# Residual update of eight chunks: five adds on GpSimd and three on VectorE, instead of four and four

## The reference

```python
def _rmsnorm(x, g):
    xf = x.astype(jnp.float32)
    y = xf * lax.rsqrt(jnp.mean(xf * xf, axis=-1, keepdims=True) + EPS)
    return (y * g.astype(jnp.float32)).astype(x.dtype)

def _pre(x, g, mod, k):
    return _rmsnorm(x, g) * (1.0 + mod[:, 3 * k + 1][:, None]) + mod[:, 3 * k][:, None]

def _post(x, y, g, mod, k, weight):
    return x + weight * mod[:, 3 * k + 2][:, None] * _rmsnorm(y, g)

x = _post(x, _swiglu(_pre(x, g[0], mod_lat, 0), ffn1_gu[l], ffn1_down[l]), g[1], mod_lat, 0, 0.5)
```

## Time and profile before

| | us |
|---|---|
| median of 3 runs | 2696.45 (2695.09 to 2696.85) |
| the profiled execution | 2699.14 |
| span of its trace | 2697.3 |
| PE busy | 2620.2 (97%) |
| DVE busy | 1641.0 (61%) |
| POOL busy | 827.6 (31%) |
| ACT busy | 718.1 (27%) |

### The profile page before, as it was taken

One profiled execution on the slowest core, in us unless ns is written; L12 is line 12 of the kernel. 1 busy time (PEld: TensorE's weight loads), 2 busy tenths in 40 slices (PEclk: granted clock), 3 DMA queues, 4 the chain that ended last, 5 costly groups with the idle time before them and its releaser, 6 DMA issues.

```text
span 2697.3 us, 40977 instructions
## 1 busy us (share of the span) xinstructions
PE 2620.2 (97%) x17108; PEld 2446.3 (91%) x17108; DVE 1641.0 (61%) x2293; ACT 718.1 (27%) x1022; POOL 827.6 (31%) x1292
## 2 busy tenths in 40 slices
PE   6999999999999999999999999999999999999998
PEld 4999999998969899999999899999999868788886
DVE  5688878867563677667666733443434684644444
ACT  5212212123314422112112412122113414322222
POOL 1268876832140200000000248677651051000001
PEclk9999999999999999999999999999999999999999
DMA  9534443453464143443442322222223556233331
GB/s 333 141 118 160 142 155 130 164 178 128 127 182 143 40 133 119 132 125 117 132 127 85 92 83 84 92 87 92 92 94 128 174 166 188 71 94 101 95 94 63
DMA packets 340466, 337.19 MB, mean 125 GB/s; under 512 B 52529, under 2 KB 311225, under 8 KB 336697
## 3 DMA queue, kind: packets, MB, share of 16 engines
q1 hardware_dynamic: 279224, 204.07, 25.8%
q10 hardware_dynamic: 51840, 77.07, 8.5%
q0 software_dynamic: 9216, 53.42, 5.3%
HBM read 290.02 MB, written 44.50 MB: 124 GB/s over the span
## 4 chain that ended last, share of the span: by engine, by line
PE 87%; DVE 7%; ACT 2%; issue 2%; POOL 1%; DMA 1%; SPq 0%; DVEq 0%; ACTq 0%; POOLq 0%
PE ps L464 78%; PE ps L1630 2%; POOL xT L1198 1%; PE ps L1655 1%; DVE hL L1403 1%; DVE tmpN L1399 1%; PE ps L1218 1%; PE ps L1233 1%; PE ps L613 1%; ACT wH L449 1%; PE ps L1644 1%; DMA xin<-in_x_dram 1%; PE ps L965 1%; PE ps L984 0%; DVE adaW L571 0%
## 5 line engine op out<-in xcount | busy, mean ns | idle before, releaser
L464 PE MATMUL ps<-hH,wH 128*128 128x384 f32 (+1 forms) x2928 | 1013.0, 346 | 6.6 <-DVE hL L1403 3.8
L464 PE MATMUL ps<-hH,wL 128*128 128x384 f32 (+1 forms) x2928 | 1004.9, 343 | 0.0
L464 PE MATMUL ps<-hL,wH 128*128 128x384 f32 (+1 forms) x2928 | 1004.5, 343 | 0.0
L456 DVE TENSOR_TENSOR wL<-raw,wH 128x1024 fp32r<-128x1024 f32 x300 | 389.3, 1309 | 476.1 <-ACT wH L449 474.7
L464 PEld LDWEIGHTS ps<-hH,wH 128*128 128x128 f32 x2928 | 550.1, 188 | 32.4 <-DVE hL L1403 6.3
L464 PEld LDWEIGHTS ps<-hH,wL 128*128 128x128 f32 x2928 | 550.1, 188 | 18.3
L464 PEld LDWEIGHTS ps<-hL,wH 128*128 128x128 f32 x2928 | 550.3, 188 | 17.8
L464 PE MATMUL ps<-midH,wH 128*128 128x384 f32 (+1 forms) x1232 | 424.9, 345 | 3.7 <-DVE yT L877 3.3
L449 ACT ACTIVATE wH<-raw 128x1024 fp32r<-128x1024 f32 x300 | 310.7, 1050 | 423.6 <-PE ps L464 406.8
L464 PE MATMUL ps<-midH,wL 128*128 128x384 f32 (+1 forms) x1232 | 422.2, 343 | 0.0
L464 PE MATMUL ps<-midL,wH 128*128 128x384 f32 (+1 forms) x1232 | 422.1, 343 | 0.0
(11 more groups left out here) (271 smaller groups left out, 2295.9 us busy)
## 6 DMA issues: line engine op xcount, KB each, us to landing
raw<-in_ffn_gu_dram SPq DMA_DIRECT2D x176, 512.0 KB, 3.8
adaW<-in_w_ada_dram ACTq DMA_DIRECT2D x40, 1536.0 KB, 6.9
raw<-in_ffn_down_dram SPq DMA_DIRECT2D x88, 512.0 KB, 3.6
x_d<-xT POOLq DMA_DIRECT2D x4, 3072.0 KB, 10.5
xT<-x_d POOLq DMA_DIRECT2D x4, 3072.0 KB, 11.5
W_d<-gW POOLq DMA_DIRECT2D x16, 512.0 KB, 3.6
VT_d<-gVT ACTq DMA_DIRECT2D x16, 512.0 KB, 3.0
raw<-in_w_in_dram SPq DMA_DIRECT2D x16, 512.0 KB, 5.4
```

The costliest lines, as they stand in the source:

```text
L456: nc.vector.tensor_tensor(wL[:, n % SPLIT_SLOTS, :], raw[:, n % RAW_SLOTS, :], wH[:, n % SPLIT_SLOTS, :].bitcast(f32), ALU.subtract).then_ ...
L464: ins = nc.tensor.matmul(dst, a, b, start=first and n == 0, stop=last and n == 3 * len(pairs) - 1)
```

## The change

The list of POOL's chunks gets a fifth. `DVE_CHUNKS` follows from it.

```diff
-    POOL_CHUNKS = (0, 1, 2, 3)
+    POOL_CHUNKS = (0, 1, 2, 3, 4)
     DVE_CHUNKS = tuple(m for m in range(KC) if m not in POOL_CHUNKS)
```

## The result

| | before | after |
|---|---|---|
| median of 4 runs, us | 2696.11 (2695.09 to 2696.85) | 2728.97 (2727.46 to 2729.49) |
| the profiled execution | 2699.14 | 2728.87 |
| its span | 2697.3 | 2727.1 |
| mean granted clock of TensorE | 0.996 | 0.990 |

The change makes the kernel slower: ratio 1.0121, 95% interval 1.0104 to 1.0139. That is some 33 us between the medians and 29.7 between the two profiled executions, where 4.7 were forecast. That is far outside the predicted range.

A forecast was written before the change was run, and what follows sets the result against it. With POOL's residual adds on the path to a PE busy 97%, the terms 3.40 + 0.81 + 0.52 = +4.73 us put the median at 2701.2 us, from 2696.45; the range was 2698.3 to 2705.5.

The forecast's parts named there:

- What bounds the kernel: PE is busy 97% of the span; POOL's residual adds in the norm stages are on the path to the end.
- off the path: Rival: POOL's fifth add costs the norm stages nothing, the end gives 0.60 back at best; 2695.9 us, chance 0.05.
- The handover between the two adders: Adds of DVE and POOL exclude each other; the waiting engine goes next, a blocked POOL instruction ending 1.71 after its release.
- The first four norm stages, 768 columns: POOL's add of chunk 4 goes first by 0.04; PE's row sums come 0.85 later per stage, +3.40 in all.
- DVE first in all stages: Rival: DVE's chunk 5 goes ahead of POOL's chunk 4, +1.71 per 768-column stage; 2704.6 us, chance 0.24 (some or all).
- The second mixer's stage: Norm stage of 512 columns: DVE goes first, POOL's chunk 4 follows, PE's row sums start later: +0.81.
- the end of the program: PE waits for all eight chunks; DVE first, then POOL's chunk 4, then DVE's last two adds: +0.52.
- POOL first everywhere: Rival: POOL goes first in every stage, as it has no wait between its adds; +4.35, 2700.8 us, chance 0.14.
- No blocking: Rival: the two engines' adds do not block each other; +3.11, 2699.6 us, chance 0.10.
- The list of what would show it wrong: POOL's fifth add much over 1.8, a falling granted clock, or ACT's square of chunk 4 less than 0.8 later.

The follow-up runs named there:

- e4: Changed kernel, but DVE waits once for all eight scaled chunks ahead of its three adds, instead of before each; 2704.2 us, ratio 1.0025.
- e1: Changed kernel, but DVE waits after each of its adds until that add has finished; 2715.22 us, ratio 1.0063.
- e6: Changed kernel, but DVE's weight split waits until POOL has done its five adds; 2721.74 us, ratio 1.0095.
- e7: Changed kernel, but DVE's second add waits for all eight scaled chunks and its third for nothing; 2724.99 us, ratio 1.0103.
- e5: Changed kernel with 16 filler matmuls instead of one on PE after chunk 3 in the 768-column stages; 2717.56 us, ratio 1.0075.
- e9: Changed kernel, one wait for all eight scaled chunks ahead of DVE's adds, POOL's fifth add held back by waits; 2713.31 us, ratio 1.0058.
- f3: Changed kernel, pause put before the last chunk's scaling on DVE, POOL's fifth add held back by two memsets; 2720.61 us, one run.
- f1: Changed kernel, no wait between DVE's first and second add, no pause ahead, POOL's fifth add held back by two memsets; 2727.83 us, one run.
- f2: Changed kernel, pause ahead of DVE's first add, waits between adds kept, POOL's fifth add held back by two memsets; 2712.55 us, one run.

## Why the prediction was wrong, point by point

- **What bounds the kernel.** Right: the adds are on the path, and chunk 4 sets when PE goes on. The rival *off the path* is out; e4 shows 0.84 lost for 0.85 worked out.
- **The handover between the two adders.** Half right. The engines exclude each other, and a released POOL add needs 1.65 (forecast 1.71). With the roles changed the turn came as assumed: in the narrow stage DVE, waiting since 2333.00, went ahead of POOL's fifth. Wrong was what the prediction drew from "POOL, which was waiting, came between", namely that a waiting POOL gets the next turn after one instruction of DVE. It rested on the mixer, where DVE's multiplies stand behind a pause, and no row showed a request to an unbroken run of DVE. There the waiting POOL does not get the next turn. The Trainium skill says in "SBUF — State Buffer", section "Who interferes with whom", that whoever issues first has the shared pair for the whole instruction. Taken one instruction at a time, which the section does not spell out, that would give POOL its turn after DVE's first add; the trace agrees for one instruction, but not for a run without a pause, where the other is out for all of it (5.48). The measurement decides.
- **The first four norm stages, 768 columns.** This is the step that failed, on three counts. *Who goes first*: POOL was given it for a lead of 0.04. In the run the lead was 0.00 in the first stage and 0.07 in the third, and DVE went first in all four. A lead of 0.08 or 0.09 lost in the third stages of e1, e6 and e7, and 0.08 won in that of e5; 0.11 to 0.20 won in all four stages of e4. *How long the loser waits*: not one add (+1.71) but three and a split: chunk 4 came +4.52 late. *What the idle time does*: priced at nothing for 0.8 us, which e4 bears out (0.81 idle, clock 1.00), but with 4.5 us idle the clock fell. The trace of before had a warning that the prediction passed over: at the end of the program PE idles 5.20, and the transposes behind it begin at a clock of 0.50 (window below). Sum: 4 x 4.54 = 18.2 for the blocking, 11.6 for the clock, together 29.8 in place of 3.40 (the stages themselves: 29.66).
- **The second mixer's stage** and **the end of the program.** Right: +0.75 and +0.46 for 0.81 and 0.52. Here DVE's first add was itself blocked by POOL's fourth, and POOL got the next turn, as assumed. The transposes' 0.34 more was not foreseen; the same 32 matmuls took 5.49 (e7) to 6.59 (e4) over the runs, at a mean clock of 0.61 in before and 0.57 in after, so it need not be the change's.
- **The rivals.** *DVE first in all stages* had the right order of the two, at 2704.6 us; e1 and e9 are that case, and took 9 to 11 us more than it said, mostly because their 1.6 to 1.8 us of idle PE already brought the clock down in three stages of four (7.8 and 6.6 us of it in their traces). *POOL first everywhere* occurred in no run: in e4 POOL was first at 768 columns, but DVE at 512, as in the forecast. *No blocking* fell with after's first row.
- **The list of what would show it wrong** named POOL's fifth add and the granted clock, and both showed it. The range did not follow: it let each stage fail by one add at most, though how long a blocked engine can be kept out was a quantity without a row, and 3.8 us of DVE's work stood behind the request (659.07 to 662.90).

The window of before at the end of the program, from the start of the transposes on, with the granted clock third from the end:

```profile
2686.70:2688.70 2.00, 1.99 (x10) 2.00 (x11) 0.00 (x0) 0.02 (x1) 0.00 (x0) 0.50 0.04 8
```

What stays open: why an unbroken run keeps POOL out and a pause of 0.12 opens it, even 1.06 ahead, and how far back a pause may lie. In after's first stage DVE's stream ran unbroken from 651.06 to 662.90. Nor is a pause always needed: in the narrow stages DVE's stream has none, but its first add was held up by POOL's fourth, and POOL got the next turn. The runs show when it happens, not the mechanism.

Five and three would lose without any of this, as e4 shows: of two engines that exclude each other, the chunk goes to the one that takes 1.77 instead of 0.87 for it. No version was faster than before.

## What to carry to other kernels

Before moving work between two engines, look in a trace for places where their instructions meet: if they exclude each other, the sum of both counts, and work belongs on the faster. A blocked engine can be out for the other's whole run of back-to-back instructions, not for one, so where a result of the blocked engine is on the path, either let it ask first with a clear lead or break the other's run with a wait. And price the idle time of PE behind it at both levels of its clock.

## What the runs showed of the hardware that I had not expected

- A pause of 0.12 us in DVE's stream is worth 2.8 us to POOL's add: 5.48 without (after), 2.65 with (e1); 5.18 without (f1), 2.44 with (f2).
- At the handover a lead of 0.07 to 0.09 in the records did not give POOL the turn in four third stages (after, e1, e6, e7), but 0.08 did in one (e5); from 0.11 on it always did (e4).
- PE idle 0.81 us did not move the clock (e4); 1.64 and 1.76 did so in three of four stages (e1, e9), 1.76 in all four of f3; 3.35 and 4.49 in every one (e6, after). 3.84 us of fillers with 1.16 of idle behind them held it (e5).
